# Modulation rows of a fused decoder layer by TensorE in four column strips, and low parts of h by Vector

## What is computed

```python
mod = jax.nn.silu(c) @ w_ada[l] + b_ada[l]
shift1, scale1, gate1, shift2, scale2, gate2 = [m[:, None, :] for m in jnp.split(mod, N_MOD, axis=-1)]
h = rms_norm(x, norm_attn[l]) * (1.0 + scale1) + shift1
proj = h @ w_in[l]
```

## Time and profile before

| | us |
|---|---|
| median of 3 runs | 1460.69 (1459.41 to 1463.49) |
| profiled execution, its own time | 1459.45 |
| its span | 1457.50 |
| PE busy in the span | 1343.0 |
| DVE busy | 839.3 |
| ACT busy | 552.4 |
| POOL busy | 86.2 |
| mean granted clock | 0.977 |

### The profile page before, as it was taken

How to read it: one execution, slowest core, us unless ns; L and a number is a source line. 1 busy time by engine, 2 the same in 40 slices (tenths; PEclk the granted TensorE clock), 3 DMA queues, 4 the chain that set the end, 5 groups by cost and what they waited for, 6 DMA issues and landing times.

```text
span 1457.5 us, 17346 instructions
## 1 busy us (share of the span) xinstructions
PE 1343.0 (92%) x6720; PEld 1123.0 (77%) x6720; DVE 839.3 (58%) x1229; ACT 552.4 (38%) x887; POOL 86.2 (6%) x84
## 2 busy tenths in 40 slices
PE   2899999787989998878999899999999998999998
PEld 1788878676878877767877688888888886887886
DVE  8633354577556898865348766566665543334333
ACT  3512212456435676852127333333333322232231
POOL 1600200131000000010000000000000000001001
PEclk9999999998999999988999999999999999999999
DMA  9052423000001000210104222221222225446443
GB/s 380 28 224 108 173 88 134 1 0 1 0 2 44 2 0 1 79 67 1 58 29 173 87 87 87 87 80 67 79 79 87 87 73 201 136 147 231 168 150 123
DMA packets 34204, 132.98 MB, mean 91 GB/s; under 512 B 3536, under 2 KB 3664, under 8 KB 32592
## 3 DMA queue, kind: packets, MB, share of 16 engines
q1 hardware_dynamic: 31792, 123.54, 23.8%
q0 software_dynamic: 2336, 8.39, 1.6%
HBM read 112.00 MB, written 19.92 MB: 91 GB/s over the span
## 4 chain that ended last, share of the span: by engine, by line
PE 73%; DVE 15%; issue 5%; ACT 3%; POOL 2%; DMA 1%; DVEq 0%; SPq 0%; ACTq 0%; POOLq 0%
PE ps L1840 26%; PE ps L1481 15%; PE ps L1470 9%; PE ps L1472 8%; PE ps L1471 8%; DVE left L1206 4%; PE ps L1677 2%; PE ps L1699 2%; DVE acc L969 1%; PE ps L1686 1%; DVE beta L1210 1%; PE ps L1666 1%; POOL rstd L487 1%; DVE sqs L954 1%; DMA t_spill_d<-tst 1%
## 5 line engine op out<-in xcount | busy, mean ns | idle before, releaser
L1470 PE MATMUL ps<-TH,dWH 128*128 128x512 f32 x352 | 137.9, 392 | 6.6 <-DVE dWL L1438 5.7
L1471 PE MATMUL ps<-TL,dWH 128*128 128x512 f32 x352 | 137.7, 391 | 0.0
L1472 PE MATMUL ps<-TH,dWL 128*128 128x512 f32 x352 | 137.5, 391 | 0.0
L1840 PE MATMUL ps<-h2H,slH 128*128 128x512 f32 x320 | 125.2, 391 | 3.9 <-ACT s L874 3.9
L1840 PE MATMUL ps<-h2L,slH 128*128 128x512 f32 x320 | 125.2, 391 | 0.0
L1840 PE MATMUL ps<-h2H,slL 128*128 128x512 f32 x320 | 125.0, 391 | 0.0
L1436 DVE TENSOR_TENSOR TL<-traw,TH 128x512 fp32r<-128x512 f32 x44 | 30.5, 693 | 137.8 <-ACT TH L895 137.8
L857 ACT ACTIVATE slH<-ssum 128x512 fp32r<-128x512 f32 x80 | 50.4, 632 | 146.2 <-PE ps L1840 96.1
L895 ACT ACTIVATE TH<-traw 128x512 fp32r<-128x512 f32 x44 | 27.8, 631 | 168.2 <-PE ps L1472 156.5
L1206 DVE TENSOR_TENSOR_SCAN left<-omb 128x127 f32<-128x127 f32 (+3 forms) x64 | 86.3, 1349 | 7.0 <-ACT omb L765 6.7
L948 DVE TENSOR_TENSOR WL<-raw,WH 128x1024 fp32r<-128x1024 f32 x30 | 38.3, 1280 | 85.5 <-ACT WH L541 85.5
(11 more groups left out here) (299 smaller groups left out, 3081.3 us busy)
## 6 DMA issues: line engine op xcount, KB each, us to landing
ada<-ada SPq DMA_DIRECT2D x12, 2048.0 KB, 8.2
draw<-down SPq DMA_DIRECT2D x44, 512.0 KB, 3.6
sraw<-gu SPq DMA_DIRECT2D x20, 1024.0 KB, 6.0
traw<-t_spill_d SPq DMA_DIRECT2D x44, 256.0 KB, 3.8
t_spill_d<-tst SPq DMA_DIRECT2D x20, 512.0 KB, 3.0
raw<-win SPq DMA_DIRECT2D x18, 512.0 KB, 3.7
x_in<-xT SPq DMA_DIRECT2D x4, 1024.0 KB, 8.7
raw<-wout SPq DMA_DIRECT2D x8, 512.0 KB, 4.0
```

The costliest lines, as they stand in the source:

```text
L1470: mm(out, lh, rh, start=first, stop=False)
L1471: mm(out, lh, rl, start=False, stop=False)
L1472: return mm(out, ll, rh, start=False, stop=last)
L1840: last = mm(ps[:, Q_BANK[q], :], l[q][:, w], r[:, c, :], start=(c == 0 and k == 0 and q not in (Q_G2, Q_S4)), stop=(c == 3 and k == 2), sk ...
```

## The change

- PE makes the modulation row of a group: for each of the eight parts of the contraction an fp32 matmul whose stationary side is `silu_w`, 32 columns of which only the first is not zero, and whose moving side is the 128x512 block of `ada1`. Part k goes to the column strip k mod 4, partitions 32c to 32c + 31 of a PSUM bank (`mod1_rows`). DVE copies the bank to `acc1` (`mod1_copy`), and PE sums it over partitions with the ones (`mod1_columns`). `silu_w` is cleared by POOL and filled by ACT with a second activation.
- ACT makes `hH` directly from the normalized tokens, and then h. DVE subtracts for `hL` (`h_low`); POOL no longer does.
- The projection's first two tiles: the products with `hH` of a block come first, then the modulation group, then the lagging block of tile 1, then the small matmuls, then the product with `hL`.
- 40 matmuls of constants stand behind PE's turning of the sums.
- The angles take two operations instead of sixteen; the diagonals two instead of eight, each with its own semaphore step and its own broadcast; the two weight splits move behind the reduction and behind the diagonals.

The diff, without the list of semaphore names and one shifted count:

```diff
 LAG = 3
+WARM = 40
 BLOCKS = [NT - i for _, i in UNITS]
...
     silu_c = at("silu_c", [P, KD], F32, 6.125)
+    silu_w = at("silu_w", [P, KD, 32], F32, 138)
     mod1 = at("mod1", [P, 16], F32, 6.25)
...
+        pool.memset(silu_w[:], 0.0).then_inc(sem["silu_zero"], 1)
         fill(pool.memset(ident[:], 0.0))
...
-        for j in range(KD):
-            pool.wait_ge(sem["hH_done"], j + 1)
-            nc.gpsimd.tensor_tensor(hL[:, j, :], x_in[:, j, :], hH[:, j, :], ALU.subtract).then_inc(sem["hL_done"], 1)
...
         A(silu_c[:], cols[:, C_C:C_C + KD], ACT.Silu).then_inc(sem["silu_c_done"], 1)
+        act.wait_ge(sem["silu_zero"], 1)
+        A(silu_w[:, :, 0:1], cols[:, C_C:C_C + KD].unsqueeze(2), ACT.Silu).then_inc(sem["silu_c_done"], 1)
         for j in range(KD):
...
             act.wait_ge(sem["a1_done"], j // 2 + 1)
+            A(hH[:, j, :], x_in[:, j, :], ACT.Identity, scale=a1[:, j:j + 1], bias=mod1[:, j:j + 1]).then_inc(sem["hH_done"], 1)
             A(x_in[:, j, :], x_in[:, j, :], ACT.Identity, scale=a1[:, j:j + 1], bias=mod1[:, j:j + 1]).then_inc(sem["h_done"], 1)
-            act.wait_ge(sem["h_done"], j + 1)
-            A(hH[:, j, :], x_in[:, j, :], ACT.Copy).then_inc(sem["hH_done"], 1)
...
         fr = rows[:, R_FREQ:R_FREQ + HALF]
-        for tt in range(NT):
-            ch(V.tensor_scalar(ang[:, tt, 0, :], fr, pos_f[:, tt:tt + 1], None, ALU.mult))
-            ch(V.tensor_scalar(ang[:, tt, 1, :], fr, pos_f[:, tt:tt + 1], None, ALU.mult))
+        for c in range(2):
+            ch(V.tensor_tensor(ang[:, :, c, :], fr.unsqueeze(1).broadcast_to([P, NT, HALF]), pos_f[:].unsqueeze(2).broadcast_to([P, NT, HALF]), ALU.mult))
         ch.sync()
...
-        def adaln1(g, between=None):
-            if g == 0:
-                dve.wait_ge(sem["silu_c_done"], 1)
+        def mod1_copy(g):
+            dve.wait_ge(sem["ada_part"], g + 1)
             if g >= 2:
                 dve.wait_ge(sem["mod1_mm"], g - 1)
-            dve.wait_ge(ada1_in[g], 16)
-            a = acc1[g % 2]
-            ch(V.tensor_scalar(a[:], ada1[:, g, 0, :], silu_c[:, 0:1], None, ALU.mult))
-            for k in range(1, KD - 1):
-                if k == 4 and between:
-                    between()
-                ch.sync()
-                ins = V.scalar_tensor_tensor(a[:], ada1[:, g, k, :], silu_c[:, k:k + 1], a[:], ALU.mult, ALU.add)
-                if k < KD - 2:
-                    ch(ins)
-            ins.then_inc(sem["acc1_done"], 1)
-        wsplit(0, 0)
-        wsplit(1, 1)
+            V.tensor_copy(acc1[g % 2][:], ps[:, 4 + g % 2, :]).then_inc(sem["acc1_done"], 1)
...
         V.tensor_scalar(ms[:, 0, :], rss[:], 1.0 / D, EPS, ALU.mult, ALU.add).then_inc(sem["stat_ms"], 1)
-        diagonals(0, 0, diag1)
-        adaln1(0)
+        wsplit(0, 0)
+        dve.wait_ge(sem["stat_r"], 1)
+        for hf in range(2):
+            t = slice(4 * hf, 4 * hf + 4)
+            V.tensor_tensor(diag1[:, t, :], ident[:].unsqueeze(1).broadcast_to([P, 4, P]), rms[:, 0, t].unsqueeze(2).broadcast_to([P, 4, P]), ALU.mult).then_inc(sem["stat_diag"], 1)
+        wsplit(1, 1)
...
-        dve.wait_ge(sem["stat_bc"], 1)
+        def normalize(j):
+            V.tensor_tensor(x_in[:, j, :], x_in[:, j, :], pair(6), ALU.mult).then_inc(sem["xr_done"], 1)
+        def h_low(j):
+            dve.wait_ge(sem["hH_done"], j + 1)
+            dve.wait_ge(sem["h_done"], j + 1)
+            V.tensor_tensor(hL[:, j, :], x_in[:, j, :], hH[:, j, :], ALU.subtract).then_inc(sem["hL_done"], 1)
+        mod1_copy(0)
+        dve.wait_ge(sem["stat_bc"], 2)
+        normalize(0)
+        scale_shift(0)
+        normalize(1)
         for g in range(KD // 2):
-            for j in (2 * g, 2 * g + 1):
-                V.tensor_tensor(x_in[:, j, :], x_in[:, j, :], pair(6), ALU.mult).then_inc(sem["xr_done"], 1)
+            if 2 * g + 2 < KD:
+                normalize(2 * g + 2)
+            h_low(2 * g)
             if g + 1 < KD // 2:
-                adaln1(g + 1, lambda: scale_shift(g))
-            else:
-                scale_shift(g)
+                mod1_copy(g + 1)
+                normalize(2 * g + 3)
+            h_low(2 * g + 1)
+            if g + 1 < KD // 2:
+                scale_shift(g + 1)
...
             g = 0 if k < 3 else 1
-            dve.wait_ge(sem["stat_bc"], 2 + g)
+            dve.wait_ge(sem["stat_bc"], 3 + g)
             V.scalar_tensor_tensor(lowT[:, k, :], lowT[:, k, :], cols[:, C_QA + k:C_QA + k + 1], pair(4 + 2 * g), ALU.mult, ALU.mult).then_inc(sem["low_done"], 1)
...
-            pe.wait_ge(sem["stat_diag"], k + 1)
+            pe.wait_ge(sem["stat_diag"], k + 2)
             for hf in halves:
...
-        def adaln1(g):
+        def mod1_rows(g):
...
                 pe.wait_ge(sem["stat_ms"], 1)
+                pe.wait_ge(sem["silu_c_done"], 2)
             if g >= 2:
             pe.wait_ge(ada1_in[g], 16)
-            pe.wait_ge(sem["silu_c_done"], 1)
+            for k in range(KD):
+                c = k % 4
+                last = mm(ps[32 * c:32 * c + 32, 4 + g % 2, :], silu_w[:, k, :], ada1[:, g, k, :], start=(k < 4), stop=(k >= 4))
+            last.then_inc(sem["ada_part"], 1)
+        def mod1_columns(g):
...
             for m in range(4):
-                w = slice(m * P, (m + 1) * P)
-                mm(ps[:, 4 + g % 2, m:m + 1], ada1[:, g, KD - 1, w], silu_c[:, KD - 1:KD], start=True, stop=False, skip_group_check=True)
-                last = mm(ps[:, 4 + g % 2, m:m + 1], acc1[g % 2][:, w], ones[:, 0:1], start=False, stop=True, skip_group_check=True)
+                last = mm(ps[:, 4 + g % 2, m:m + 1], acc1[g % 2][:, m * P:(m + 1) * P], ones[:, 0:1], start=True, stop=True)
             last.then_inc(sem["mod1_mm"], 1)
-        broadcast(0, diag1, 6)
-        adaln1(0)
+        for _ in range(WARM):
+            mm(ps[:, 0, 0:P], identb[:], identb[:], start=True, stop=True)
+        mod1_rows(0)
+        for hf in range(2):
+            pe.wait_ge(sem["stat_diag"], hf + 1)
+            mm(ps[:, 6 + hf, :], ones[:], diag1[:, 4 * hf:4 * hf + 4, :].rearrange("p t n -> p (t n)"), start=True, stop=True).then_inc(sem["stat_bc"], 1)
+        mod1_columns(0)
...
         for n in range(KD + LAG):
+            if n < KD:
+                w = slice(n * P, (n + 1) * P)
+                pe.wait_ge(sem["hH_done"], n + 1)
+                for k, l in enumerate((WH, WL)):
+                    for hf in range(2):
+                        mm(ps[:, hf, :], l[0][:, w], hH[:, n, 512 * hf:512 * hf + 512], start=(n == 0 and k == 0), stop=False)
             if n % 2 == 0 and n // 2 + 1 < KD // 2:
-                adaln1(n // 2 + 1)
+                mod1_rows(n // 2 + 1)
+            if n >= LAG:
+                for hf in range(2):
+                    last = half_chunk(1, 2, hf, n - LAG, hH, hL)
+            if n % 2 == 0 and n // 2 + 1 < KD // 2:
+                mod1_columns(n // 2 + 1)
             if n < KD:
                 for hf in range(2):
-                    last = half_chunk(0, 0, hf, n, hH, hL)
+                    last = mm(ps[:, hf, :], WH[0][:, w], hL[:, n, 512 * hf:512 * hf + 512], start=False, stop=(n == KD - 1))
                 if n == KD - 1:
                     last.then_inc(sem["pe_tile"], 1)
-            if n >= LAG:
-                for hf in range(2):
-                    last = half_chunk(1, 2, hf, n - LAG, hH, hL)
         last.then_inc(sem["pe_tile"], 1)
```

4 lines of the change are left out of this document (2 added, 2 removed).

## The result

The changed kernel takes 1450.66 us (median of 6 runs, 1449.16 to 1454.03), the kernel before 1462.17 in the same comparison (median of five runs; a sixth, 1569.4 us, was a slow run and isn't counted). The ratio of the means is 0.9926, with a 95% interval of 0.9909 to 0.9944: faster by 0.74%, about 10.8 us. The time is what rival 1 of the prediction gave (1449.9), not its forecast (1458.6). It lies inside the stated range, 1448.5 to 1470, only because that range was drawn wide enough to take in rivals 1 and 2. The profiled execution took 1449.16 against 1459.45, its span is 1447.3 against 1457.5.

What follows compares the result with a forecast made beforehand. DVE's serial sum bounds the stage; nine-pass steps of 9.6 us put the last `hL` at 68.2, tile 3 at 85.8 instead of 87.89, 2.1 us earlier: 1458.6 us predicted, range 1448.5 to 1470.

Steps and rivals of the forecast that it cites:

- rival 1: Modulation groups on PE: four strips run at once, 4 passes (1.7 us), 1449.9; four to six passes had chance 0.30.
- rival 2: Modulation groups on PE: strips don't run at once, 16 passes, tile 3 9.8 us later, 1470.5; chance 0.17.
- likeliest case: Nine passes per modulation group, 3.84 us, giving 1458.6; alone it reaches from 1456.5 to 1460.5; chance 0.36.
- nine passes: Each modulation group on PE: a matmul's second pass overlaps only the next matmul's first, 3.84 us.
- 5.2 passes: Modulation group on PE: estimate scaling the skill page's 3.07 times to four strips; sum near 1452.
- the sum: Projection's start: start, steps and tail added up to the last low part at 68.2 and tile 3 at 85.8.
- pitch: Time between a1 operations, DVE's scale and shift for two blocks of h: 9.6 us forecast, against 9.77 before.
- The cover of the second split: DVE, 26.1 to 27.3 us: the second weight split runs while its next work, group 0's copy, isn't ready.
- The chain of 17.52 us behind the last low part: After the last `hL`: POOL clears acc2, SP loads 2 MB, DVE adds, then splits tile 3's weights.
- PE's backlog: PE's own queued work before tile 3, the other bound on its start: 84.7 in the forecast, 76.2 in rival 1.
- rival 3: PE's clock stays at or falls to the lower level while strips run: some 8 us worse, 1466.6; chance 0.12.

Runs made afterwards that it cites:

- after: The changed kernel itself, in its profiled execution, beside the kernel before: median 1450.66 us, ratio 0.9926.
- marks: Changed kernel with a semaphore increment on each of a group's eight strip matmuls, not only the last: 1452.52 us in one run.
- whole_array: Changed kernel with `silu_w` 128 columns wide instead of 32, so a group's eight matmuls use the whole array: 1470.77 us, ratio 1.0063.
- split_first: Changed kernel with the weight split of tile 3 ahead of the long addition on DVE's queue: 1447.78 us, ratio 0.9911.
- uneven_strips: Changed kernel with parts 0 to 4 in strip 0, parts 5 to 7 in strips 1 to 3, each matmul incrementing: 1463.46 us in one run.
- changed_again: The changed kernel without an edit, run again beside variants on their chip: 1451.70 us, ratio 0.9940.
- statistics_undone: Changed kernel with the old sixteen angle multiplications, eight diagonals and both weight splits ahead of the reduction: 1453.40 us in one run.
- no_constants: Changed kernel without the 40 constant matmuls (WARM = 0): 1451.84 us, ratio 0.9929.

## Why the forecast missed and rival 1 held

The range held, but the likeliest case didn't: it had a chance of 0.36 and stood at 1458.6, 8 us above the measured 1450.66; rival 1 had 0.30.

**The step that failed** is the price of eight matmuls in four strips. I took nine passes, 3.84 us, because the two passes of one matmul stand next to each other in the written order and a pass was thought to hold up everything behind it. Measured are four, 1.85 us. The starts in after refute it: the four strips start within 20 ns. marks shows why the order in the rows misled me: the first passes of four matmuls run ahead of their second ones. All sixteen starts within 1.9 us is the sign that the prediction had named for rival 1; they lie within 1.33 (24.32 to 25.65), four at once and the next four 0.43 us later. What spoke for rival 1, the figures of the Trainium skill ("TensorE: Matmul & The Clock Gate", "Measured speedup vs the span model"), was nearer than my reading of the row order. The 5.2 passes came from its 3.07 times, which it gives for four row tiles; its 2.38 is for three column tiles, and it has no row for four of them. The kernel has 4 passes (3.7 times in whole_array against after).

With that one term exchanged the sum holds:

| | rival 1 | measured |
|---|---|---|
| first a1 done | 31.2 | 29.80 |
| pitch | 7.5 | 7.78, 7.73, 7.93 |
| last a1 | 53.7 | 53.24 |
| last low part | 59.5 | 59.31 |
| tile 2 starts | 65.3 | 65.03 |
| tile 3 starts | 77.1 | 76.99 |
| tile 3 earlier by | 10.8 | 10.90 |
| median of the runs | 1449.9 | 1450.66 |

Two misses cancel: the start came 1.4 us earlier than rival 1 had it, the three pitches together are 0.9 longer. That the last low part fits to 0.2 us is luck to that extent.

**The start.** The adds end at 19.01 for 19.3; x landed a little earlier. The diagonals are ready at 26.56 for 26.1, since POOL's power takes 2.51 us beside the split (forecast: free). The Trainium skill has the reason on "SBUF — State Buffer", "Who interferes with whom": a Vector instruction with two inputs in SBUF contends with a GpSimd instruction that reads it. The rows agree, 2.51 us with the split beside it and 1.68 without. The constants take 3.4 us (20.9 to 24.3), not 4.3, since the fast pace came at 23.2; I had 26.5, with 22.5 as a bound. In other executions it came from 22.4 to 26.0. The first group then ran fast as a whole, and the broadcast is done at 28.15. The cover of the second split held: it ends at 27.70, and normalization can't start before 28.15.

**The pitch.** The step from 29.64 to 37.42 is: a1, handoff and hH 1.64, PE's four matmuls 1.09, strips and handoff 1.99, copy 0.61, normalization 1.13, low part 1.13, scale and shift 0.19. In the forecast's grouping the first two were 1.3 and 0.91, 0.5 too short; the last two 1.52 against 1.32.

**What was right, and what was left out.** DVE's serial sum was the bound before, and removing it moved the bound to a chain across three engines (ACT, PE, DVE). But the pitch of 9.77 holds for two steps only. The third took 4.76, which the prediction didn't say; its forecast of three steps of 9.6 would have made the steps themselves 4.5 us slower than before, made up by the earlier start and a shorter tail. The chain of 17.52 us behind the last low part measured 17.53 in after (17.1 to 18.5 in the variants that keep it), and made tile 3's weights and not PE's backlog the limit, as rival 1 said; split_first removes that limit and finds PE's backlog 1.2 us earlier. In after the wait was 0.92 us, forecast about 1. Sixteen passes give 1470.8, as rival 2 said. Low parts on DVE, forecast at 1.15 us in the pitch, are 1.13.

**The clock** (rival 3) is partly real: it falls around the first step in seven of eleven executions, at 1.4 to 2.7 us and not the 4 a step of nine passes would have cost. It didn't in the execution whose timeline is shown, which is luck for the comparison with rival 1.

**Where the 10.9 us are from.** The strips against whole passes are 21.2 us of tile 3's start, some 19.5 without the lower clock in whole_array; the statistics 0.5 to 0.9; the constants 0.4 and 1.2 in two pairs, and nothing where the clock rose late; the low parts nothing that the traces show. These come from comparisons of single executions and don't add up to 10.9: whole_array has all the other parts and still starts tile 3 10.3 us later than the kernel before, so each part's worth depends on what bounds the stage without it.

## What to carry to other kernels

A sum over the contraction that keeps Vector busy can go to TensorE even with one useful column, if it is shared evenly among the four column strips: without strips it lost 10 us here, with them it gained 11. Two written orders of the strips cost the same; an even share matters, and with an uneven one each strip needs its own increment. Compare single executions from a point that the edit can't touch: here the start and the clock moved by more than the smaller parts of the change were worth. When a bound moves to a chain of short handoffs, the next gain is in the order: issuing each group one block earlier, with the split ahead of the long addition, took the ratio from 0.9926 to 0.9864.

## What the runs showed of the hardware

- Sixteen fp32 passes of 512 columns in four column strips take 1.85 us, on the whole array 6.93. Four strips start within 20 or 40 ns, by the written order. About 0.09 of the 1.85 lie between the last pass in strips and the next on the whole array.
- Across strips, passes run out of the written order: parts 5 to 7 of uneven_strips start 0.85 us ahead of part 4 and increment ahead of it, but start only when three passes are left waiting in strip 0. Whether the engine or the compiled order does it isn't shown.
- POOL's power on 8 elements per partition takes 2.51 us beside a two-input subtraction on DVE, 1.68 without it.
- Behind one and the same gap of 1.88 us in PE the granted clock fell to 0.50 in one execution of the changed kernel and not in another. That the gap is the cause isn't shown.
- The clock rose at 22.4 us in changed_again and at 26.0 in statistics_undone, both with forty constants from 20.8 and 21.8 us on; the forty took 3.2 and 4.4 us by that.
- At the start of these programs the column of the granted clock reads 1.00 because the trace has no record of it yet (the first is at 27.54 us in no_constants). Sixteen passes took 3.64 us for 1.92 under that 1.00; up to the first record the pace of the passes tells the level.
